# mLSTM values on one core: fp32 products of weights and values replaced by pairs of split fp32r products

## The chip, the core and the metric

The kernel runs on one core of one Trainium2 chip. The metric is the device time of one execution in microseconds. A run here is a timed execution; a profile is one execution taken by the hardware profiler. The engines are TensorE (PE, with its weight loads as PEld), VectorE (DVE), ScalarE (ACT), GpSimd (POOL) and SyncE (SP, which issues the DMAs). They run their own instruction streams in order and wait for each other on semaphores.

## The reference, cut to what matters

The reference is one layer of a hybrid encoder: 512 tokens, 1024 channels, three branches (stick-breaking attention, mLSTM, attention into a memory), gates, an output projection and a layer of 16384 small experts. Only the mLSTM branch bears on the change. It is written chunk by chunk; over the whole sequence it amounts to this, for each of 4 heads of width 128:

```python
dmat = where(causal, bcum[..., :, None] - bcum[..., None, :] + ig[..., None, :], -inf)
w    = einsum('bhtd,bhsd->bhts', q, k) * exp(dmat - m_t[..., None])
num  = einsum('bhts,bhse->bhte', w, v)
den  = sum(w, axis=-1)
h    = num / maximum(abs(den), exp(-m_t))[..., None]
```

The change is in the product of the weighted scores `w` with the values `v`. A column of ones beside the values gives `den` from the same product.

## The kernel before

**Layout.** 512 tokens are 4 tiles of 128 partitions. The projections of the normed input come as items: an item is 16 products of 128 x 512 whose weights (1024 columns) were split into a high part by ACT (`high_w`, L1337) and a low part by POOL (`low_ws`, L491; some by DVE), both fp32r. fp32r is the form that TensorE takes as one product per instruction; a plain fp32 matmul is carried out as two. `SPREAD` and `KEEP` are scale factors that make the high part lose its low bits when it is written as fp32r, so that the low part is the exact rest.

**Stages.** The transposes and most projections end near 166 us. Then come four pairs of attention heads (`for p in range(PAIRS)`, 166 to 255 us), between whose steps PE runs gate items 4 to 16; then mLSTM (255 to 284 us); then the memory attention, the branch projections, and from about 330 us to the end the experts.

**mLSTM.** PE does, for heads (0, 1) and then (2, 3): `ml_scores` of both heads (L991, fp32r, 16 products for each head pair of narrowing width), `gate_item(17)` or `gate_item(19)`, `ml_values` of both heads (L1002), and a further gate item, 18 or 20. The scores stay in PSUM as the causal part only: 1280 columns for each head. Ahead of the values DVE makes the exponents (`decay`, L1900), ACT their exponential (L1470), POOL masks the diagonal blocks (`keep_causal`, L480), and DVE multiplies by the scores (`weigh`, L1951) and signals `w_ready`. `ml_values(h)` waits for `w_ready` and forms 10 products of 128 x 129 for each head: weights `ew[h]`, moving operand `ml_v4`, both plain fp32. `divide(h)` (L1961 to L1966) reads the result, and `num_out` lets PE write the next scores into the same banks.

**What sets the order.** Each engine's stream is written out by hand. The order around the change: on DVE `take_gate` (L1834) copies a gate item out of PSUM, and PE waits for it before the gate item after next; `split_low` (L1908, L1911) makes the low parts of the mLSTM queries and keys, without which `ml_scores` can't run. On ACT `split_high(p)` stands at the end of attention pair p, `high_ws` makes the high part of the next item's weights. On POOL `low_ws` follows the items in order. Lines L1877 to L1960 of the DVE stream hold the attention pairs' loop and the decays.

## Time and profile before

| | |
|---|---|
| time, median of 3 runs | 1466.06 us (1465.7 to 1466.77) |
| the profiled execution's own time | 1466.18 us |
| its span, first to last instruction | 1464.5 us |
| PE busy | 1455.2 us, 99% of the span |
| DVE, ACT, POOL busy | 76%, 51%, 29% |
| mean granted TensorE clock | 0.999 of full speed |

The time is the span and 1.7 us around it. "Busy" of PE is from a product's start to the end of its last result, so that neighbours overlap: the distance from one product's start to the next, not the length of one, tells what a product costs. The rows of a timeline merge neighbours of one line: start, time from the first start to the last end, and how many.

### The profile page before, as it was taken

To read this page: it belongs to the slowest core of one execution; us is meant where nothing else is said; L and a number is where in the kernel's file an instruction comes from. 1 tells how busy PE (TensorE), PEld (TensorE's weight loads), DVE (VectorE), ACT (ScalarE), POOL (GpSimd) and SP (SyncE) were. 2 spreads that over 40 slices of the span, in tenths; PEclk is the share of its full clock that TensorE was granted. 3 is DMA by queue.
4 is the path that set the end of the run, shared out by engine and by line. 5 is a ranking of instruction groups with operands and counts; after the bars stand their busy time and mean duration, and the time that the engine had idled before them with its cause. 6 is when DMAs were issued, how large, how long until landed. Compare 5 with 4: busy or idle time off the path is not lost.

```text
span 1464.5 us, 22288 instructions
## 1 busy us (share of the span) xinstructions
PE 1455.2 (99%) x7466; PEld 1208.1 (82%) x7466; DVE 1107.4 (76%) x1903; ACT 747.2 (51%) x955; POOL 424.6 (29%) x200
## 2 busy tenths in 40 slices
PE   9999999999999999999999999999999999999999
PEld 8888777878788888888888888888888888888887
DVE  5977688867589999996999997346666666666665
ACT  6444677477645454554556555454444444444442
POOL 5866435436546687884000000000000000000000
PEclk9999999999999999999999999999999999999999
DMA  7544533538433666666888888988888888888883
GB/s 239 172 144 144 202 123 108 174 121 300 152 116 115 219 219 208 215 209 206 299 304 303 310 297 305 321 285 287 297 297 281 296 283 296 284 293 286 292 286 139
DMA packets 166705, 345.16 MB, mean 236 GB/s; under 512 B 13420, under 2 KB 78956, under 8 KB 164336
## 3 DMA queue, kind: packets, MB, share of 16 engines
q1 hardware_dynamic: 166640, 344.32, 69.2%
q8 instruction: 37, 0.61, 0.2%
q14 instruction: 28, 0.23, 0.0%
HBM read 268.76 MB, written 75.51 MB: 235 GB/s over the span
## 4 chain that ended last, share of the span: by engine, by line
PE 86%; DVE 10%; ACT 2%; POOL 1%; issue 0%; DMA 0%; SPq 0%; ACTq 0%; POOLq 0%
PE ps L1229 32%; PE ps L1220 25%; PE ps L747 9%; PE ps L770 6%; PE ps L1258 4%; PE ps L1089 3%; DVE top_lists L2156 1%; DVE top_lists L2149 1%; POOL u_r L538 1%; PE ps L954 1%; PE ps L735 1%; DVE top_in L2150 1%; DVE top_lists L2153 1%; DVE top_lists L2146 1%; PE ps L938 1%; PE ps L964 1%
## 5 line engine op out<-in xcount | busy, mean ns | idle before, releaser
L1220 PE MATMUL ps<-hT_r,u_r 128*128 128x512 f32 x2048 | 470.6, 391 | 0.1
L1229 PE MATMUL ps<-v_r,w_pairs 128*128 128x512 f32 x2036 | 461.7, 389 | 0.0
L1220 PEld LDWEIGHTS ps<-hT_r,u_r 128*128 128x128 f32 x2048 | 382.8, 188 | 79.7 <-POOL u_r L538 0.5
L1229 PEld LDWEIGHTS ps<-v_r,w_pairs 128*128 128x128 f32 x2036 | 382.3, 188 | 79.2
L491 POOL TENSOR_TENSOR w_r<-w_raw,w_r 128x1024 fp32r<-128x1024 f32 x85 | 217.0, 2558 | 182.5 <-ACT w_r L1337 105.0
L2295 DVE TENSOR_TENSOR v_r<-vraw,v_r 128x1024 fp32r<-128x1024 f32 x128 | 156.9, 1226 | 148.7 <-ACT v_r L1675 148.7
L1675 ACT ACTIVATE v_r<-vraw 128x1024 fp32r<-128x1024 f32 x128 | 135.7, 1061 | 253.6 <-PE ps L1229 249.0
L1622 ACT ACTIVATE act_stage<-ps 128x512 f32<-128x512 f32 x128 | 76.6, 598 | 226.5 <-PE ps L1220 226.4
L538 POOL TENSOR_TENSOR u_r<-uraw,u_r 128x1024 fp32r<-128x1024 f32 x60 | 172.9, 2892 | 46.6 <-ACT u_r L1603 46.4
L1337 ACT ACTIVATE w_r<-w_raw 128x1024 fp32r<-128x1024 f32 x95 | 100.0, 1059 | 112.2 <-PE ps L747 44.9
L1603 ACT ACTIVATE u_r<-uraw 128x1024 fp32r<-128x1024 f32 x128 | 134.9, 1054 | 15.8 <-DMA uraw<-in_u 12.9
L747 PE MATMUL ps<-xT_r,w_r 128*128 128x512 f32 x592 | 141.2, 393 | 0.0
L747 PEld LDWEIGHTS ps<-xT_r,w_r 128*128 128x128 f32 x592 | 109.8, 188 | 23.3 <-issue 0.7
L2257 DVE TENSOR_TENSOR u_r<-uraw,u_r 128x1024 fp32r<-128x1024 f32 x68 | 82.6, 1223 | 56.1 <-ACT u_r L1603 55.7
L2291 DVE TENSOR_TENSOR w_f<-act_in,g_in 128x512 f32<-128x512 f32 x128 | 87.6, 685 | 6.1 <-issue 6.1
L2298 DVE SCALAR_TENSOR_TENSOR w_pairs<-w_pairs,w_f 128x512 fp32r<-128x512 f32 x128 | 87.5, 684 | 0.0
L1677 ACT ACTIVATE w_pairs<-w_f 128x512 fp32r<-128x512 f32 x128 | 78.6, 614 | 3.8 <-DVE w_f L2291 3.8
L1645 ACT ACTIVATE stage<-ps 128x1024 f32<-128x1024 f32 x64 | 61.8, 1019 | 5.0 <-PE ps L1258 5.0
L1258 PEld LDWEIGHTS ps<-onehots 128*128 128x128 bf16 x1024 | 58.8, 97 | 4.2 <-issue 4.2
L1258 PE MATMUL ps<-onehots 128*128 128x128 bf16 x1024 | 61.6, 219 | 0.0
L770 PE MATMUL ps<-w_r,xT_r 128*128 128x512 f32 x256 | 58.2, 389 | 0.0
L770 PEld LDWEIGHTS ps<-w_r,xT_r 128*128 128x128 f32 x256 | 48.1, 188 | 10.0
(272 smaller groups left out, 1538.6 us busy)
## 6 DMA issues: line engine op xcount, KB each, us to landing
uraw<-in_u SPq DMA_DIRECT2D x128, 512.0 KB, 4.8
vraw<-in_v SPq DMA_DIRECT2D x128, 512.0 KB, 5.2
w_raw<-in_w SPq DMA_DIRECT2D x100, 512.0 KB, 3.5
acts_out<-act_stage SPq DMA_DIRECT2D x128, 256.0 KB, 2.3
gates<-stage SPq DMA_DIRECT2D x16, 2048.0 KB, 7.4
g_in<-gates SPq DMA_DIRECT2D x64, 512.0 KB, 6.4
act_in<-acts_out SPq DMA_DIRECT2D x128, 256.0 KB, 5.2
gates_pre<-pre_stage SPq DMA_DIRECT2D x24, 256.0 KB, 2.4
```

What stands on the lines that cost most here:

```text
L491: pool.tensor_tensor(wr4[:, n % 2, 1, :], raw3[:, n % 4, :], wr4[:, n % 2, 0, :].bitcast(F32), ALU.subtract).then_inc(w_lo_ready, 1)
L538: pool.tensor_tensor(u2[n % 4][:, 1, :], u_raw[n % 4], u2[n % 4][:, 0, :].bitcast(F32), ALU.subtract).then_inc(u_lo, 1)
L747: ins = pe.matmul(bank(b), slot_of(s)[:, w, k * P:(k + 1) * P], act[:, w, k, :], start=k + w == 0, stop=k == KD - 1 and w == 1)
L770: ins = pe.matmul(bank(b0 + t), act[:, w, 2 * j + k, t * P:(t + 1) * P], wr4[:, s, w, k * BANK:(k + 1) * BANK], start=j + k + w == 0, stop ...
L1220: ins = pe.matmul(bank(s % 2), u2[s][:, w, k * P:(k + 1) * P], hr4[:, w, k, :], start=i == 0, stop=i == 15, skip_group_check=True)
L1229: ins = pe.matmul(bank(2 * q + h), w2[:, s, w, q * P:(q + 1) * P], v2[s][:, w, h * BANK:(h + 1) * BANK], start=start and w == 0, stop=stop ...
L1258: ins = pe.matmul(ps[:, at:at + P], oh_tiles[3 * s][:, q // PAIR, :, q % PAIR], oh_tiles[3 * s + 1 + w][:, q // PAIR, :, q % PAIR], start= ...
L1337: act.activation(slot_of(n)[:, 0, :], raw3[:, q, :], ACT.Copy, scale=KEEP).then_inc(w_hi_ready, 1)
L1603: act.activation(u2[s][:, 0, :], u_raw[s], ACT.Copy, scale=KEEP).then_inc(u_hi, 1)
L1675: act.activation(v2[s][:, 0, :], vr[:, s, :], ACT.Copy, scale=KEEP).then_inc(v_hi, 1)
L2291: dve.tensor_tensor(wf[:, s % 2, :].rearrange("p (b t) -> p b t", t=BLK), ai3[:, s, :].rearrange("p (b t) -> p b t", t=BLK), g4[:, par, :, ...
L2295: dve.tensor_tensor(v2[s][:, 1, :], vr[:, s, :], v2[s][:, 0, :].bitcast(F32), ALU.subtract).then_inc(v_lo, 1)
```

## The change

The values' products become fp32r. Weights are split as `ew_hi`, `ew_lo`; values as `ml_v_high`, `ml_v_low`. For each of the 40 blocks there are two products that add up in PSUM: high weights by high values and low weights by low values; the scale of the weights' high part carries the cross terms. The width goes from 129 to 130 columns (two columns of ones). The values are split on ACT and POOL in three runs of 3, 7 and 6 head tiles behind attention pairs 0, 1 and 2. The weights of a head are split once they are made: ACT writes the high part (`high_e`), DVE the low part in place (`low_e`), and `w_ready` is now signalled by `low_e`. On ACT, `high_e(0)` and `high_e(1)` stand ahead of the weights of items 18 and 19, `high_e(2)` and `high_e(3)` between those of items 20 and 21. On DVE `decay(3)` and `take_gate(16)` change places. Some semaphores are merged, a few tiles move by 16 or 288 columns, and two rows change places in memory, so that a split run of values can lie where they were.

```diff
+V_RUNS = (3, 7, 6)
 ...
+            def low_v(i):
+                pool.wait_ge(v_split_hi, i + 1)
+                pool.tensor_tensor(v_run(ml_v_low, i), v_run(ml_v, i), ml_v_high[i].bitcast(F32),
+                                   ALU.subtract).then_inc(v_split_lo, 1)
+
-            low_ws(I_G + GATES_IN_KV, 14)
+            low_ws(I_G + GATES_IN_KV, 5)
+            for p in range(PAIRS - 1):
+                low_v(p)
+                low_ws(I_G + GATES_IN_KV + 5 + 3 * p, 3)
 ...
             def ml_values(h):
+                pe.wait_ge(v_split_lo, len(V_RUNS))
                 pe.wait_ge(w_ready, h + 1)
                 for t in range(TT):
-                    at = (h % 2 * 3 + t // 2) * BANK + (t % 2) * (HD + 1)
+                    at = (h % 2 * 3 + t // 2) * BANK + (t % 2) * (HD + 2)
                     for kt in range(t + 1):
-                        ins = pe.matmul(ps[:, at:at + HD + 1], part(ew[h], kt, t, t + 1), ml_v4[:, kt, h, :],
-                                        start=kt == 0, stop=kt == t)
+                        for w, weights in enumerate((ew_hi[h], ew_lo[h])):
+                            ins = pe.matmul(ps[:, at:at + HD + 2], part(weights, kt, t, t + 1), (v_high, v_low)[w](kt, h),
+                                            start=kt + w == 0, stop=kt == t and w == 1)
 ...
+            def high_v(i):
+                act.activation(ml_v_high[i], v_run(ml_v, i), ACT.Copy, scale=KEEP).then_inc(v_split_hi, 1)
+
+            def high_e(h):
+                act.wait_ge(weighed, h + 1)
+                at_least(act, num_done, h - 1)
+                act.activation(ew_hi[h], ew[h], ACT.Copy, scale=1.0 / SPREAD).then_inc(weighed_hi, 1)
 ...
                 if p < PAIRS - 1:
                     split_high(p)
+                    if p == 0:
+                        act.wait_ge(n_out, 2 * TT)
+                        act.wait_ge(row_in, 32)
+                    high_v(p)
 ...
+            for h in range(2):
+                high_e(h)
             high_ws(I_G + 18, I_G + 19)
             act.activation(ml_o, ml_o, ACT.Sigmoid).then_inc(ml_factors, 1)
-            high_ws(I_G + 20, I_G + 21, I_G + 22)
+            high_ws(I_G + 20)
+            for h in range(2, MLH):
+                high_e(h)
+            high_ws(I_G + 21, I_G + 22)
 ...
             decay(2)
+            decay(3)
             take_gate(16)
-            decay(3)
 ...
-                dve.scalar_tensor_tensor(out=ew[h], in0=region(h % 2), scalar=HD_SCALE * SPREAD, in1=ew[h],
-                                         op0=ALU.mult, op1=ALU.mult).then_inc(w_ready, 1)
+                dve.scalar_tensor_tensor(out=ew[h], in0=region(h % 2), scalar=HD_SCALE * SPREAD * SPREAD, in1=ew[h],
+                                         op0=ALU.mult, op1=ALU.mult).then_inc(weighed, 1)
+
+            def low_e(h):
+                dve.wait_ge(weighed_hi, h + 1)
+                dve.scalar_tensor_tensor(out=ew_lo[h], in0=ew_hi[h].bitcast(F32), scalar=1.0 - SPREAD, in1=ew[h],
+                                         op0=ALU.mult, op1=ALU.add).then_inc(w_ready, 1)
 ...
             for h in (0, 2):
                 weigh(h)
                 weigh(h + 1)
+                low_e(h)
+                low_e(h + 1)
                 take_gate(17 + h)
```

On PE, from the last products of the scores of heads 0 and 1 to the gate item behind their values, before (`L1002` is `ml_values`):

```order
L991 MATMUL ps<-projT_r 128x512
L991 MATMUL ps<-projT_r 128x384
L991 MATMUL ps<-projT_r 128x256
L991 MATMUL ps<-projT_r 128x128
L747 MATMUL ps<-xT_r,w_r 128x512 x16
L1002 MATMUL ps<-ml_v,work 128x129 x20
L747 MATMUL ps<-xT_r,w_r 128x512 x16
```

The same place after the change (`L1029` is `ml_values`; the pair of rows repeats 20 times):

```order
L1016 MATMUL ps<-projT_r 128x128
L772 MATMUL ps<-xT_r,w_r 128x512 x16
L1029 MATMUL ps<-ml_v_high,lk_hi 128x130
L1029 MATMUL ps<-ml_v_low,lk_lo 128x130
L1029 MATMUL ps<-ml_v_high,lk_hi 128x130
L1029 MATMUL ps<-ml_v_low,lk_lo 128x130
```

20 fp32 instructions, which the trace shows as 40 products, became 40 fp32r instructions; what stands around them is the same.

On DVE, from `decay(2)` through the weighing of heads 0 and 1 to `split_low(2)`, before (`L1900` is `decay`, `L1834` `take_gate`, `L1951` `weigh`, `L1908` and `L1911` `split_low`):

```order
L1900 TENSOR_SCALAR work<-r_all,key_cols 128x128
L1834 TENSOR_TENSOR pre_stage<-ps,rstd_b 128x512
L1900 TENSOR_SCALAR work<-r_all,key_cols 128x512
L1900 TENSOR_SCALAR work<-r_all,key_cols 128x384
L1900 TENSOR_SCALAR work<-r_all,key_cols 128x256
L1900 TENSOR_SCALAR work<-r_all,key_cols 128x128
L1951 SCALAR_TENSOR_TENSOR work<-ps,work 128x1280 x2
L1834 TENSOR_TENSOR pre_stage<-ps,rstd_b 128x512
L1908 SCALAR_TENSOR_TENSOR projT_r<-projT_r,projT 128x512
```

And after (`L1946` is `decay`, `L1880` `take_gate`, `L1997` `weigh`, `L2002` `low_e`, `L1954` `split_low`):

```order
L1946 TENSOR_SCALAR work<-r_all,key_cols 128x512
L1946 TENSOR_SCALAR work<-r_all,key_cols 128x384
L1946 TENSOR_SCALAR work<-r_all,key_cols 128x256
L1946 TENSOR_SCALAR work<-r_all,key_cols 128x128
L1880 TENSOR_TENSOR pre_stage<-ps,rstd_b 128x512
L1997 SCALAR_TENSOR_TENSOR work<-ps,work 128x1280 x2
L2002 SCALAR_TENSOR_TENSOR lk_lo<-lk_hi,work 128x1280 x2
L1880 TENSOR_TENSOR pre_stage<-ps,rstd_b 128x512
L1954 SCALAR_TENSOR_TENSOR projT_r<-projT_r,projT 128x512
```

`take_gate(16)` moved behind `decay(3)`, and the two `low_e` stand between `weigh` and `take_gate(17)`.

On ACT, from `split_high(3)` to the copies of the memory attention's queries, after the change (`L1511` is the exponential, `L1486` `high_e`, `L1364` `high_w`, `L1517` the sigmoid):

```order
L1511 ACTIVATE work<-work 128x1280 x3
L1486 ACTIVATE lk_hi<-work 128x1280 x2
L1364 ACTIVATE w_r<-w_raw 128x1024 x2
L1517 ACT_TABLE_LOAD
L1517 ACTIVATE ml_o<-ml_o 128x2048
L1364 ACTIVATE w_r<-w_raw 128x1024
L1486 ACTIVATE lk_hi<-work 128x1280 x2
L1364 ACTIVATE w_r<-w_raw 128x1024 x2
```

Both `L1486` rows are new; the weights of items 18 and 19, and of item 21, now stand behind them.

## Rows read from the trace of the kernel before

**Rows 1.** The page: busy time by engine, and the last chain's shares by engine.

```profile
PE 1455.2 (99%) x7466; PEld 1208.1 (82%) x7466; DVE 1107.4 (76%) x1903; ACT 747.2 (51%) x955; POOL 424.6 (29%) x200
...
PE 86%; DVE 10%; ACT 2%; POOL 1%; issue 0%; DMA 0%; SPq 0%; ACTq 0%; POOLq 0%
```

**Rows 2.** Groups by line and shape, 150 to 330 us: count, busy us, mean ns.

```profile
L1002 PE MATMUL ps<-ml_v,work 128*128 128x129 f32 x80 | 9.3, 275 | 0.0
...
L1002 PEld LDWEIGHTS ps<-ml_v,work 128*128 128x128 f32 x80 | 9.2, 192 | 0.2
```

**Rows 3.** Timeline of PE in mLSTM: start us, length us, line, names, count.

```profile
257.75 3.89 PE L747 MATMUL ps<-xT_r,w_r 128*128 128x512 f32 x16
261.48 4.63 PE L1002 MATMUL ps<-ml_v,work 128*128 128x129 f32 x40
265.86 3.91 PE L747 MATMUL ps<-xT_r,w_r 128*128 128x512 f32 x16
...
275.85 4.63 PE L1002 MATMUL ps<-ml_v,work 128*128 128x129 f32 x40
280.23 3.91 PE L747 MATMUL ps<-xT_r,w_r 128*128 128x512 f32 x16
```

**Rows 4.** Timeline of PE, fp32r products of the last attention head, narrow ones among them.

```profile
244.16 0.22 PE L954 MATMUL ps<-lk_hi,rest_r 128*128 128x128 f32 x1
244.22 0.28 PE L954 MATMUL ps<-lk_hi,tri_r 128*128 128x128 f32 x1
244.33 0.44 PE L954 MATMUL ps<-lk_lo,tri_r 128*128 128x512 f32 x1
244.62 0.34 PE L954 MATMUL ps<-lk_lo,ones_r 128*128 128x384 f32 x1
```

**Rows 5.** Timeline of PE's weight loads in the same stretch.

```profile
244.05 0.19 PEld L954 LDWEIGHTS ps<-lk_hi,rest_r 128*128 128x128 f32 x1
244.16 0.19 PEld L954 LDWEIGHTS ps<-lk_hi,tri_r 128*128 128x128 f32 x1
244.28 0.19 PEld L954 LDWEIGHTS ps<-lk_lo,tri_r 128*128 128x128 f32 x1
244.39 0.19 PEld L954 LDWEIGHTS ps<-lk_lo,ones_r 128*128 128x128 f32 x1
```

**Rows 6.** Timeline of DVE in mLSTM.

```profile
256.05 1.36 DVE L1900 TENSOR_SCALAR work<-r_all,key_cols 128x512 f32<-128x512 f32 x4
257.33 2.88 DVE L1951 SCALAR_TENSOR_TENSOR work<-ps,work 128x1280 f32<-128x1280 f32 x2
...
262.29 2.81 DVE L1908 SCALAR_TENSOR_TENSOR projT_r<-projT_r,projT 128x512 fp32r<-128x512 f32 x1
...
271.10 2.89 DVE L1951 SCALAR_TENSOR_TENSOR work<-ps,work 128x1280 f32<-128x1280 f32 x2 [0.32 <-PE ps L991]
276.05 0.69 DVE L1834 TENSOR_TENSOR pre_stage<-ps,rstd_b 128x512 f32<-128x512 f32 x1 [2.06 <-PE ps L747]
```

**Rows 7.** Timeline of ACT in mLSTM.

```profile
257.45 1.28 ACT L1470 ACTIVATE work<-work 128x1280 f32<-128x1280 f32 x1 [1.38 <-DVE work L1900]
258.63 1.04 ACT L1337 ACTIVATE w_r<-w_raw 128x1024 fp32r<-128x1024 f32 x1
...
274.27 1.06 ACT L1337 ACTIVATE w_r<-w_raw 128x1024 fp32r<-128x1024 f32 x1 [5.17 <-PE ps L747]
```

**Rows 8.** Timeline of POOL in mLSTM.

```profile
259.83 4.71 POOL L491 TENSOR_TENSOR w_r<-w_raw,w_r 128x1024 fp32r<-128x1024 f32 x2
```

**Rows 9.** Timelines of ACT and POOL at the end of attention pair 2.

```profile
227.65 0.62 ACT L1449 ACTIVATE projT_r<-projT 128x512 fp32r<-128x512 f32 x1
230.85 1.24 ACT L1426 ACTIVATE work<-ps 128x1280 f32<-128x1280 f32 x1 [2.58 <-PE ps L942]
...
228.05 2.35 POOL L491 TENSOR_TENSOR w_r<-w_raw,w_r 128x1024 fp32r<-128x1024 f32 x1 [0.56 <-PE ps L747]
```

**Rows 10.** Instructions on the tile r_all: its DMA's issue, us.

```profile
L592 SPq DMA_DIRECT2D r_all<-acts_out x1: 432/432/432, 151.8 to 151.8; - x1
```

More of the change, by code:

```diff
@@ L276, in build, with v_high, v_low, v_run @@
         sb_v3 = sb_v.rearrange("p (t c) -> p t c", c=512)
-        ml_v4 = ml_v.rearrange("p (t h c) -> p t h c", t=TT, c=HD + 1)
+        ml_v4 = ml_v.rearrange("p (t h c) -> p t h c", t=TT, c=HD + 2)
+        def v_high(t, h):
+            n = t * MLH + h
+            i = 0 if n < V_RUNS[0] else 1 if n < V_RUNS[0] + V_RUNS[1] else 2
+            at = (n - sum(V_RUNS[:i])) * (HD + 2)
+            return ml_v_high[i][:, at:at + HD + 2]
+        def v_low(t, h):
+            return ml_v_low[:, (t * MLH + h) * (HD + 2):(t * MLH + h + 1) * (HD + 2)]
+        def v_run(whole, i):
+            return whole[:, sum(V_RUNS[:i]) * (HD + 2):sum(V_RUNS[:i + 1]) * (HD + 2)]
         ml_o3 = ml_o.rearrange("p (t c) -> p t c", c=512)
@@ L294, in build @@
         ew = lk + aw
+        ew_hi = [lkr[0][h % 2] for h in range(MLH)]
+        ew_lo = [lkr[1][0], lkr[1][1], aw_r[:, 0:CAUSAL], aw_r[:, CAUSAL:2 * CAUSAL]]
         probs = [work[:, 0:1024], work[:, 1024:2048]]
@@ L300, in row @@
             return rows[0:4, n * T:(n + 1) * T]
-        r_abs, r_f, r_lf, r_b, r_a, r_max, r_m, r_zero = (row(n) for n in range(8))
+        r_abs, r_f, r_lf, r_b, r_a, r_m, r_max, r_zero = (row(n) for n in range(8))
         r_all3 = r_all.rearrange("p (h t) -> p h t", t=T)
@@ L1403, in _ @@
             high_w(I_N + 2, (I_N + 2) % 4)
-            act.activation(r_abs, r_abs, ACT.Ln, bias=1.0).then_inc(if_ln, 1)
+            act.activation(r_abs, r_abs, ACT.Ln, bias=1.0).then_inc(if_made, 1)
             for b in range(4):
```

81 lines of the change are left out of this document (42 added, 39 removed).

## The prediction, as it was made before the changed kernel ran

> **What bounds the kernel now.** I read the page first [rows 1]: PE is busy 99% of the span and holds 86% of the chain that ended last. So time is won only if PE's own stream gets shorter, and lost only if PE is made to wait. The groups by line and shape come next [rows 2]: the products to be replaced are 80 records of 128 x 129 in fp32, two for each of the 40 instructions, each with a weight load of its own. The timeline of PE [rows 3] gives their real price. The values of heads 0 and 1 start at 261.48 and the gate item behind them at 265.86: 4.38 us for 40 products, 0.110 us each; heads 2 and 3 take the same 4.38 us. Together 8.76 us, and no stage of the change touches PE elsewhere. Even if these products cost nothing, the kernel would win 0.6%; a measurement of this kernel can tell about 0.2%, or 2.9 us, from no change.
>
> **What the new products cost.** The program order shows 80 fp32r instructions of 128 x 130. An fp32r instruction is one record in the trace (a gate item has 16 instructions and 16 records [rows 3]), so 80 records replace 80 records. The only saving can come from the rate: fp32r streams its columns faster than fp32. But each product needs its own 128 x 128 weights, and these are again fp32r. What does a narrow fp32r product cost when its neighbour is narrow too? The trace of before has no long run of them, but it has pairs, at the end of each attention head's suffix sums. There the second narrow product starts 0.06 us after the first (244.16, 244.22), and the next one 0.11 us after that (244.33) [rows 4]. The weight loads of the same stretch start at 244.05, 244.16, 244.28 and 244.39 [rows 5]: 0.34 us for three, 0.113 each. The last of them could have begun at 244.33, when the product before it did, and began 0.06 us later: the load ahead of it was not done. And the 512-wide product at 244.33 takes 0.29 us to its successor at 244.62, where 512-wide ones in a gate item are (261.48 - 257.75) / 16 = 0.233 apart [rows 3]. So it, too, waited some 0.06 us for its weights. I read from this that an fp32r weight load occupies the load path for 0.11 us, whatever the product beside it, and that a run of products narrower than that (0.06 us) goes at the pace of its loads. The fp32 products of before stream for about as long as a load takes, which is why their loads are 0.11 us apart as well [rows 2, 3].
>
> The bounds for one product are then 0.107 (a little under the mean load distance) and 0.113 us. For 80 products: 8.56 to 9.04 us against 8.76, that is -0.2 to +0.3 us. I take 0.112, since three loads in a row measured it: 80 x 0.112 = 8.96, **+0.2 us**. [...]
>
> The Trainium skill has two rules here that disagree. Its page "TensorE: Matmul & The Clock Gate", section "LDWEIGHTS (loading the stationary operand)", gives a load's time as its column count over 1.2 GHz, 107 ns for 128 columns; the loads in rows 5 agree within 6 ns. The section "Back-to-back issue gap" of the same page gives 81 ns for a sustained 128-wide product with its load; the rows speak against it for fp32r, but no run of them is long, so it is a rival below.
>
> **The splits of the values.** ACT gets three copies of 390, 910 and 780 columns, POOL three subtractions of the same size. By the ACT copy of 1024 columns at 1.04 us [rows 7] the largest costs 0.9 us. They stand behind `split_high` of pairs 0 to 2, where ACT idles: in pair 2 it is free from 228.27 to 230.85, 2.58 us [rows 9], and 0.8 us are put there; pairs 0 and 1 end with the same steps and about as much room. Were this cover gone, ACT's start on the next pair would slip by up to that 0.9 us. The first copy waits for the broadcast of `r_all`, whose DMA was issued at 151.8 [rows 10], 35 us ahead of pair 0's end: nothing. On POOL a subtraction of 1024 columns takes 2.35 us [rows 9], so 0.9, 2.1 and 1.8 us, behind the low part of items 8, 11 and 14; after item 14's, at 230.40, POOL has nothing to do until ACT has made the next pair's high weights, ten us later. Queued behind `low_v` are the low weights of the next items, which have not got their high parts by then. PE's wait for `v_split_lo` is over some 29 us before it is asked. **Zero.**
>
> **The split of the weights.** This is the part on the path: `w_ready` used to follow `weigh`, and now follows `weigh`, `high_e` and `low_e`. Heads 0 and 1, walked through with durations of before: `decay(3)` (1.36 us) no longer stands between `take_gate(16)` and `weigh(0)`; it fits ahead, where DVE waited for gate item 16 to end at 255.3. `take_gate(16)`, a copy of 0.69 us, then ends near 256.8, and `weigh(0)`, which started at 257.33, can follow it [rows 6]. Two `weigh` take 2.88 us, 1.44 apart: to 258.2 and 259.7. `high_e` is an ACT pass over 1280 columns, 1.28 us [rows 7]: 258.3 to 259.6 and 259.8 to 261.0; ACT is free for it, since the exponential of head 3, which ran at 257.45, comes a good microsecond earlier with the swap. `low_e(0)` follows at 259.7 and takes as long as `weigh`, to 261.2; `low_e(1)` to 262.6. PE asks for head 0 at 261.48 and for head 1 2.2 us later at 263.7 [rows 3]. **Slack 0.3 us and 1.1 us.** Heads 2 and 3: `weigh` at 271.10 to 273.99, `high_e` to 274.0 and 275.4, `low_e` to 275.6 and 277.0; PE asks at 275.85 and 278.0: slack 0.2 and 1.0 us.
>
> **What is queued behind them.** On ACT the high weights of item 18 move from 258.63 [rows 7] to about 261.0, those of 19 to 262.0; POOL's low parts, which ran from 259.83 to 264.54 [rows 8], follow at about 262.1 to 264.5 and 266.9. Gate item 18 begins at 265.86 and needs its low part 1.9 us later; item 19 comes 6 us after it. Item 21's high part slips from 274.27 to 275.4, its gate item comes after 286. On DVE `take_gate(17)` slips by about 1 us and `split_low(2)` with it. That one is the place where two engines collide: before, the first half of `split_low(2)`, 512 columns, took 2.81 us where a copy of 512 columns takes 0.69 [rows 6], since it stood still until POOL's subtraction ended at 264.54 [rows 8]. Now item 18's subtraction ends at about the same time, so `split_low(2)` ends near 266, as before, and `divide(0)` and `divide(1)` are done near 267.7 and 269.3; PE asks for the first at 269.6 with `ml_scores(2)`, for the second and for `split_low(3)` at 270.9. `low_e` reads two tiles of SBUF and could be held up by POOL in the same way, but in both places POOL has nothing to run: item 18's subtraction needs ACT's copy, which stands behind `high_e(1)`, and item 21's that behind `high_e(3)`. **Zero, with 0.3 us to spare at the tightest.**
>
> **The sum.** 1466.18 + 0.2 = 1466.4 for an execution like the profiled one. That one was 0.1 above the median of the runs before (1466.06), so **1466.3 us** as a median: no change.
>
> **Rivals.**
> - *The products stream at their own rate.* If loads were hidden, a product would cost 0.06 us, as the second narrow one does [rows 4]: 80 x (0.110 - 0.058) = 4.2 us, 1461.9. For it: the 0.06 itself, and fp32r is what all of the big stages use. Against it: each 0.06 is followed by a 0.11 and a stretched product. Chance 0.07.
> - *A product in between*, with a load that is partly hidden: halfway, 0.085, gives 80 x 0.025 = 2.0 us, 1464.1; no row shows such a distance. The skill's 81 ns, a figure of the section named above, would make it 2.3 us, 1463.8. Chance 0.04; within 0.2% either way.
> - *Slower: load and product in turn.* If in a long run of narrow products a load could not start until the product before it has left the array, each costs a load and a product, 0.11 + 0.055 = 0.165 us: 80 x 0.055 = +4.4 us, 1470.6. It decides from 0.146 us for a product. The rows speak against it: the load at 244.16 starts with the product before it, not after [rows 4, 5]. The skill says on the page named above, Part 3, "The mechanism", that a load overlaps running products only when its row group differs; rows 4 and 5 show loads of full height that do overlap. Chance 0.03.
> - *Slower: the weights come late.* If POOL is in the way of a `low_e` for one of its subtractions (2.35 us) less the slack, PE stands for 2.0 us: 1468.2, still no change by the measure; if in both places, 1470.2. Chances 0.03 and 0.01.
> - *The change is not what it says:* the compiler carries out each fp32r product as two. Then 160 products: +9 us, 1475. The gate items speak against it. Chance 0.01.
>
> **How the numbers follow.** The forecast has 0.81. The time is its time, 1466.3. Its own spread is the -0.2 to +0.3 of the products, up to 0.5 us where a slack of 0.2 or 0.3 is used up, and the 1.1 us between the runs shown. The range reaches from 1464.5, below which stand only the hidden and the half-hidden loads (0.11), to 1468.5, above which stand loads in turn, two late weights and split products (0.05). Faster by over 0.2%: 0.07. Slower by over 0.2%: 0.03 + 0.01 + 0.01 = 0.05. Within: 0.88.
>
> **What would show it right or wrong.** In the timeline of PE after, the values should take 4.4 to 4.5 us for each head pair, with product starts and load starts both 0.11 us apart; a distance of 0.06 means the first rival, 0.165 the third. The lengths of the products should be near 275 ns although they stream half as long, because each waits for its weights. DVE's `low_e` should end 0.2 to 0.3 us before PE starts the values, and no idle row of PE should name it. `split_low(2)` should end near 266. What would make the prediction wrong: that a long run of narrow loads behaves unlike the three that I could see, or that the chain from `weigh` to `low_e` is longer than the sum of its parts by more than its slack, since PE would then stand at both places and nothing later gives it back.

## The result, and the profile after

The changed kernel takes 1468.73 us (median of 14 runs, 1466.84 to 1470.17), the kernel before, on the same chip, 1465.46 us (14 runs, 1463.45 to 1466.79). The ratio is 1.0025, with a 95% interval of 1.0018 to 1.0033: slower by a quarter of a per cent; the medians are 3.3 us apart. (The ratios in this text are those on record. They are not quotients of the medians beside them and can differ from these by some 0.05%.) The forecast was 1466.3, no change, with a range up to 1468.5. The profiled execution took 1469.57 us and has a span of 1467.8 us, 3.3 us more than before.

The page of the changed kernel, busy time by engine and the shares of the chain that ended last, against [rows 1]:

```profile
PE 1455.5 (99%) x7466; PEld 1208.2 (82%) x7466; DVE 1115.5 (76%) x1907; ACT 754.5 (51%) x962; POOL 433.6 (30%) x203
...
PE 84%; DVE 11%; ACT 2%; POOL 1%; issue 1%; DMA 0%; SPq 0%; ACTq 0%; POOLq 0%; DVEq 0%
```

PE's busy time has grown by 0.3 us only, while the span grew by 3.3: by this row 3.0 us are time in which PE stood. 2.33 of them are the wait that is shown below; 0.7 lie in the first 20 us, where PE is busy 16.30 us and was 17.01, far from the change. The chain agrees: two points went from PE to DVE and to issue. DVE is busy 8.1 us longer, ACT 7.3, POOL 9.0: the splits, and on DVE and POOL also time in which an instruction counts as busy while it is held up.

Where PE stood is seen in its timeline (start us, length us, line, names, count; in brackets the idle time ahead and what ended it). `L772` is a gate item, `L1016` `ml_scores`, `L1029` `ml_values`:

```profile
265.34 3.85 PE L772 MATMUL ps<-xT_r,w_r 128*128 128x512 f32 x16
269.18 1.49 PE L1016 MATMUL ps<-projT_r 128*128 128x512 f32 x8
273.01 1.50 PE L1016 MATMUL ps<-projT_r 128*128 128x512 f32 x8 [2.33 <-DVE projT_r L1957]
274.31 5.45 PE L772 MATMUL ps<-xT_r,w_r 128*128 128x512 f32 x16
...
284.01 3.86 PE L772 MATMUL ps<-xT_r,w_r 128*128 128x512 f32 x16
```

The same timeline, the first and last products of the values:

```profile
260.93 0.22 PE L1029 MATMUL ps<-ml_v_high,lk_hi 128*128 128x130 f32 x1
260.99 0.28 PE L1029 MATMUL ps<-ml_v_low,lk_lo 128*128 128x130 f32 x1
261.10 0.28 PE L1029 MATMUL ps<-ml_v_high,lk_hi 128*128 128x130 f32 x1
...
279.60 0.22 PE L1029 MATMUL ps<-ml_v_high,lk_hi 128*128 128x130 f32 x1
```

I compare one stretch throughout, called the stage below: from the first product of the values of heads 0 and 1 to the start of gate item 20, behind the values of heads 2 and 3. Before it is 280.23 - 261.48 = 18.75 us [rows 3], after it is 284.01 - 260.93 = 23.08: 4.33 us more. By pieces, from start to start:

| piece of the stage | before | after | difference |
|---|---|---|---|
| values of heads 0, 1 | 4.38 | 4.41 | +0.03 |
| gate item 18 | 3.75 | 3.84 | +0.09 |
| scores of heads 2, 3 | 2.51 | 5.13 | **+2.62** |
| gate item 19 | 3.73 | 5.28 | **+1.55** |
| values of heads 2, 3 | 4.38 | 4.41 | +0.03 |

So the new products cost what the old ones did. Two other things happened. Between `ml_scores(2)` and `ml_scores(3)` PE stood for 2.33 us by its timeline, waiting for `split_low(3)` on DVE (`L1957`). Then gate item 19, whose products didn't change, took 1.55 us longer. The windows of the gate item's line give the reason (stretch, its length, PE and PEld busy with counts, granted clock, DMA share, GB/s):

```profile
274.31:277.73 3.42, 3.42 (x8) 2.74 (x9) 0.50 0.73 230
277.73:279.60 1.87, 1.87 (x9) 1.31 (x7) 1.00 0.00 0
```

For the first 3.42 us, 8 products, the granted clock was 0.50, which is 1.2 GHz; after that it was back at 1.00, 2.4 GHz. 8 products in 3.42 us are 0.427 each, where products at full clock are 0.233 apart: 8 x 0.194 = 1.55 us. Before the clock fell PE had stood still for 2.33 us and then formed the eight products of `ml_scores(3)`, from 273.01 to 274.31, still at the full clock.

Why was `split_low(3)` late? DVE's timeline from `low_e` on (`L2002`; `L1880` is `take_gate`, `L1954` and `L1957` the two halves of `split_low`, `L2017` the last step of a `divide`), against [rows 6]:

```profile
259.01 2.90 DVE L2002 SCALAR_TENSOR_TENSOR lk_lo<-lk_hi,work 128x1280 fp32r<-128x1280 f32 x2
261.82 0.68 DVE L1880 TENSOR_TENSOR pre_stage<-ps,rstd_b 128x512 f32<-128x512 f32 x1
262.42 2.27 DVE L1954 SCALAR_TENSOR_TENSOR projT_r<-projT_r,projT 128x512 fp32r<-128x512 f32 x1
264.62 2.87 DVE L1957 TENSOR_TENSOR projT_r<-projT,projT_r 128x512 fp32r<-128x512 f32 x1
...
269.63 1.13 DVE L2017 TENSOR_SCALAR y_ml<-ps,den 128x128 f32<-128x128 f32 x4
270.68 1.58 DVE L1954 SCALAR_TENSOR_TENSOR projT_r<-projT_r,projT 128x512 fp32r<-128x512 f32 x1
272.18 0.68 DVE L1957 TENSOR_TENSOR projT_r<-projT,projT_r 128x512 fp32r<-128x512 f32 x1
```

And POOL's, the low weights of items 18 and 19 and then of item 20, against [rows 8]:

```profile
261.49 5.45 POOL L508 TENSOR_TENSOR w_r<-w_raw,w_r 128x1024 fp32r<-128x1024 f32 x2 [3.58 <-ACT w_r L1364]
269.34 2.37 POOL L508 TENSOR_TENSOR w_r<-w_raw,w_r 128x1024 fp32r<-128x1024 f32 x1 [2.40 <-PE ps L772]
```

Half of a `split_low` takes 0.68 us when nothing is in its way. In the stage there are four halves, and three are stretched: 2.27, 2.87 and 1.58 us. Each of their ends can be set against the end of a subtraction. Taken singly, the two that POOL's row merges last 2.65 us from 261.49 and 2.83 from 264.11. The first half ends at 264.69, 0.55 us behind the end of the first subtraction (264.14); the second at 267.49, 0.55 behind the second (266.94); and 272.26 is 0.55 behind the end of item 20's (271.71). So such a half stands until the subtraction is over and then does its own work. Before, one half was stretched, to 2.81 us, again 0.56 beyond the end of POOL's work at 264.54, and the other came behind it and took its 0.68. From its first start to its last end `split_low(2)` takes 5.1 us, before 3.4; `split_low(3)` loses 0.9 us, before nothing. That POOL is busy here is ACT's doing:

```profile
257.70 2.68 ACT L1486 ACTIVATE lk_hi<-work 128x1280 fp32r<-128x1280 f32 x2 [0.90 <-DVE work L1997]
260.29 1.99 ACT L1364 ACTIVATE w_r<-w_raw 128x1024 fp32r<-128x1024 f32 x2
```

`high_e(0)` and `high_e(1)` now stand ahead of the high weights of items 18 and 19, so that these are made from 260.29 instead of 258.63, back to back, and POOL's two subtractions start at 261.49 instead of 259.83. In this profile everything here runs 0.55 us ahead of the profile of before (the values start at 260.93, before at 261.48). Counted from the values' start, the high weights and the subtractions come 2.2 us later than before, and `split_low(2)` (262.42, before 262.29) 0.7 us later. Before, the second subtraction had begun when the first half came, and nothing stood behind it; now the first half meets the first subtraction, and the second half the second.

From the values' start to the end of `split_low(3)` it is 11.9 us, before 8.7: 3.2 more. 2.2 of them are the second half of `split_low(2)`, 0.9 are `split_low(3)`'s own wait for item 20's subtraction. Before, 0.7 us of this were slack (`split_low(3)` ended at 270.18, half of the scores was through near 270.87); the other 2.5 make up nearly all of the 2.62 us lost in the scores.

The Trainium skill has this collision on its page "SBUF — State Buffer", section "Who interferes with whom": a DVE instruction with two SBUF inputs and a GpSimd instruction that reads SBUF exclude each other, and the later one waits for the whole of the earlier. The rows above agree: both halves of `split_low` read two tiles of SBUF and are stretched, while `take_gate` and `divide`, which read PSUM, ran at their usual 0.68 and 1.13 us. It holds the other way round too: `low_e(1)` ran until 261.91, so that the first subtraction stood behind it from 261.49, and the second behind the first half: 2.65 and 2.83 us, where one alone takes 2.35 [rows 9].

### The profile page after: what moved, and what is told of

It reads as the page before. It is cut to its first block, busy times and chain, and to the rows that moved or that the text cites. A ratio compares the mean times of both kernels' runs of the same rounds, so it can differ in the third digit from the quotient of the medians.

```text
span 1467.8 us, 22293 instructions
## 1 busy us (share of the span) xinstructions
PE 1455.5 (99%) x7466; PEld 1208.2 (82%) x7466; DVE 1115.5 (76%) x1907; ACT 754.5 (51%) x962; POOL 433.6 (30%) x203
## 4 chain that ended last, share of the span: by engine, by line
PE 84%; DVE 11%; ACT 2%; POOL 1%; issue 1%; DMA 0%; SPq 0%; ACTq 0%; POOLq 0%; DVEq 0%
PE ps L1256 31%; PE ps L1247 25%; PE ps L772 9%; PE ps L795 6%; PE ps L1285 4%; PE ps L1116 3%; DVE top_lists L2209 1%; DVE top_lists L2202 1%; POOL u_r L563 1%; PE ps L979 1%; PE ps L760 1%; DVE top_in L2203 1%; DVE top_lists L2206 1%; DVE top_lists L2199 1%; PE ps L963 1%
## 5 line engine op out<-in xcount | busy, mean ns | idle before, releaser
L1364 ACT ACTIVATE w_r<-w_raw 128x1024 fp32r<-128x1024 f32 x95 | 99.8, 1058 | 105.5 <-PE ps L772 41.3
L772 PE MATMUL ps<-xT_r,w_r 128*128 128x512 f32 x592 | 142.7, 396 | 0.0
L772 PEld LDWEIGHTS ps<-xT_r,w_r 128*128 128x128 f32 x592 | 111.0, 190 | 23.6 <-issue 0.7
```

Source lines behind the costliest of these rows:

```text
L772: ins = pe.matmul(bank(b), slot_of(s)[:, w, k * P:(k + 1) * P], act[:, w, k, :], start=k + w == 0, stop=k == KD - 1 and w == 1)
L1364: act.activation(slot_of(n)[:, 0, :], raw3[:, q, :], ACT.Copy, scale=KEEP).then_inc(w_hi_ready, 1)
```

## The experiments

**Theory.** ACT's new passes shift POOL's subtractions onto `split_low(2)`; each half waits for one of them; `divide(0)`, `divide(1)` and `split_low(3)` follow late; PE stands; the clock falls. **Rivals.** (a) DVE simply has too much work in this stretch, 2.9 us of `low_e` for each pair, and the collision adds nothing; (b) the new products themselves, or the splits of the values, cost the time; (c) the slow gate item has a cause of its own, unrelated to PE's standing still.

### `split_low(2)` moved ahead

Both halves of `split_low(2)` are taken out of the stretch and put behind `minus_abs(3)`, where its inputs have long been ready. Nothing else is changed, so DVE has the same work in all.

```diff
                 minus_abs(p)
+                if p == PAIRS - 1:
+                    split_low(2)
                 take_gate(m)
 ...
-                if h == 0:
-                    split_low(2)
                 divide(h)
```

> The changed kernel with split_low(2) moved into attention pair 3, behind minus_abs(3), where DVE idled 2.2 us in the profile of before. If the loss is PE's stall ahead of ml_scores(3) and the clock that falls behind it, both go: no wait of PE for split_low, granted clock 1.00 through mLSTM, the values of heads 2 and 3 start 4.3 us earlier relative to those of heads 0 and 1 (14.4 us apart instead of 18.7), and the time is 4.3 us under the changed kernel's, about 1464.5, equal to before within 0.1%. If the loss is spread over the kernel (tiles at other places, a later start), the time stays near 1468.7.

Measured: 1464.20 us (11 runs), kernel before 1465.23 (33 runs), ratio 0.9994 (0.9985 to 1.0003). PE's timeline has the scores in one piece and the gate item at its usual length, and the granted clock over 255 to 285 us is 1.00:

```profile
268.05 2.67 PE L1016 MATMUL ps<-projT_r 128*128 128x512 f32 x16
270.56 3.89 PE L772 MATMUL ps<-xT_r,w_r 128*128 128x512 f32 x16
```

DVE's and POOL's timelines:

```profile
266.20 0.68 DVE L1954 SCALAR_TENSOR_TENSOR projT_r<-projT_r,projT 128x512 fp32r<-128x512 f32 x1
```

```profile
260.51 5.00 POOL L508 TENSOR_TENSOR w_r<-w_raw,w_r 128x1024 fp32r<-128x1024 f32 x2 [3.58 <-ACT w_r L1364]
```

The half seen here is the first of `split_low(3)`, now unhindered: POOL is done at 265.5. The stage takes 18.76 us. The whole loss is gone, 4.3 of 4.3 us in the stage. This doesn't yet separate the theory from rival (a), since the move takes at least 1.4 us of DVE work out of the stretch as well.

### The same move in the kernel before

> Control: the kernel before with the same move of split_low(2). PE waits for nothing there before, so by the theory nothing is won: time within 0.1% of before, and the move in e1 wins only because it undoes the stall. If the move is worth something by itself (over 0.15%), e1's gain can't all be put down to the stall.

Measured: 1464.55 us (11 runs) against 1465.23, ratio 0.9998 (0.9988 to 1.0007); the stage takes 18.75 us. The move by itself wins nothing. What it took away in the changed kernel was the stall, not something that was there before.

### POOL waits for `split_low(2)`

The DVE stream is the changed kernel's, word for word. Only POOL's second subtraction waits until both halves of `split_low(2)` are through.

```diff
-            low_ws(I_G + 18, I_PQ - 1 - I_G - 18)
+            low_ws(I_G + 18, 1)
+            pool.wait_ge(ml_split_lo, 6)
+            low_ws(I_G + 19, I_PQ - 1 - I_G - 19)
```

> The changed kernel with POOL waiting for split_low(2) to be done before the low part of item 19. DVE has the same work in the same order. Port theory (each half of split_low(2) stands still behind one of POOL's two subtractions in a row): the second half now takes 0.7 us instead of 2.87, divide(0) starts 2.1 us earlier, PE's stall shrinks from 2.5 us to under 0.6, the clock doesn't fall, time 3.5 to 4.3 us under the changed kernel. Queue theory (DVE simply has 2.9 us more to do ahead of split_low(2)): the stall stays over 1.5 us and the time within 1 us of the changed kernel's.

Measured: 1464.68 us (10 runs), ratio 1.0001 (0.9992 to 1.0011); stage 18.76 us. DVE's and POOL's timelines:

```profile
261.56 2.27 DVE L1956 SCALAR_TENSOR_TENSOR projT_r<-projT_r,projT 128x512 fp32r<-128x512 f32 x1
263.75 0.68 DVE L1959 TENSOR_TENSOR projT_r<-projT,projT_r 128x512 fp32r<-128x512 f32 x1
```

```profile
260.55 2.73 POOL L508 TENSOR_TENSOR w_r<-w_raw,w_r 128x1024 fp32r<-128x1024 f32 x1 [3.50 <-ACT w_r L1366]
264.74 2.40 POOL L508 TENSOR_TENSOR w_r<-w_raw,w_r 128x1024 fp32r<-128x1024 f32 x1 [1.46 <-DVE projT_r L1959]
```

This is the run that decides. DVE has the same instructions in the same order, the first half is stretched just as in the changed kernel, and only the second, 2.87 us, is back at 0.68. With these 2.2 us the 0.9 us of `split_low(3)` have gone as well (both halves take 0.68), and with them the stall. Rival (a) is out. The first half again ends 0.55 us behind its subtraction (263.83 and 263.28).

### PE kept at work while it waits

Ahead of `ml_scores(3)` PE forms ten fp32 products of constants into a free bank. They change no result.

```diff
                 at_least(pe, num_out, h - 1)
+                if h == 3:
+                    pe.wait_ge(y_out, PAIRS)
+                    for i in range(10):
+                        pe.matmul(bank(6)[:, 0:P], neg_ones[:, :], neg_ones[:, :], start=True, stop=True)
                 pe.wait_ge(ml_split_lo, 2 * h + 2)
```

> The changed kernel with 10 fp32 products of 128 x 128 of constants into a free bank, ahead of PE's wait for split_low(3): 2.2 us of work in the stall, nothing else changed. If the fall of the clock to half is caused by the stall, the clock stays at 1.00 from 273 to 279 us, gate item 19 takes 3.7 us instead of 5.3, ml_scores(3) starts where it did (within 0.1 us), and the time is 1.5 us under the changed kernel's. If the clock falls for another reason (the fp32r products at half load ahead of it), it falls again and nothing is won.

Measured: 1467.25 us (10 runs), ratio 1.0016 (1.0007 to 1.0025). PE's timeline, and the windows row of 255 to 285 us (busy time with counts of PE, PEld, DVE, ACT, POOL, granted clock, DMA share, GB/s; `L1020` is `ml_scores` here and `L1016` the filler):

```profile
270.07 1.49 PE L1020 MATMUL ps<-projT_r 128*128 128x512 f32 x8
271.71 2.50 PE L1016 MATMUL ps<-neg_ones 128*128 128x128 f32 x20
273.96 1.46 PE L1020 MATMUL ps<-projT_r 128*128 128x512 f32 x8
275.26 3.89 PE L772 MATMUL ps<-xT_r,w_r 128*128 128x512 f32 x16
```

```profile
255.00:285.00 30.00, 29.85 (x191) 26.68 (x190) 28.22 (x49) 14.76 (x12) 13.66 (x16) 1.00 0.36 114
```

`ml_scores(3)` starts no earlier than in the changed kernel, 3.89 us behind `ml_scores(2)` where it was 3.83, so the wait is all there. But the clock stays at 1.00 and gate item 19 takes 3.73 us (start to start) instead of 5.28. The stage is 21.58 us: 1.5 of the 4.3 us are won by useless work. That speaks against rival (c), but it is one profile, and the fall doesn't happen in each run of the changed kernel either (see below). The timed runs point the same way without deciding: their ratio's interval, 1.0007 to 1.0025, overlaps the changed kernel's, 1.0018 to 1.0033.

### The values' product without the split of the weights

`high_e` and `low_e` are gone; `weigh` writes fp32r directly and both products of a block use it. The split of the weights is left out, so the result has lower precision; the products and the splits of the values stay.

```diff
-            for h in range(2):
-                high_e(h)
             high_ws(I_G + 18, I_G + 19)
 ...
-                low_e(h)
-                low_e(h + 1)
 ...
-                        for w, weights in enumerate((ew_hi[h], ew_lo[h])):
+                        for w, weights in enumerate((ew_lo[h], ew_lo[h])):
```

> The changed kernel without the split of the weights: no high_e on ACT, no low_e on DVE, both products of a block take the weights as weigh writes them, in fp32r (so the split's arithmetic is left out). PE's products, the values' splits and the swap of decay(3) stay. If the products cost what fp32's did and the splits of the values are hidden, and the loss comes from the weights' split alone, the time is that of before within 0.1%, with no stall of PE. If the fp32r products or the values' splits cost something of their own, the time stays over before by that.

Measured: 1464.84 us (10 runs) against 1464.48 (15 runs), ratio 1.0004 (0.9994 to 1.0013). The values take 4.42 us per pair, PE does not wait, the stage is 18.80 us. With the change's 80 products and all of its work on the values, the time is that of before within the measurement. Rival (b) is out.

### Only ACT's passes, in the kernel before

The opposite direction: two copies of 1280 columns are put on ACT ahead of the high weights of item 18, with DVE's order of `decay(3)` and `take_gate(16)` as in the change. DVE gets no `low_e`, PE keeps its fp32 products.

```diff
             decay(2)
+            decay(3)
             take_gate(16)
-            decay(3)
 ...
+            for h in range(2):
+                act.wait_ge(w_ready, h + 1)
+                act.activation(lkr[0][h % 2], ew[h], ACT.Copy, scale=1.0 / SPREAD)
             high_ws(I_G + 18, I_G + 19)
```

> The kernel before with the swap of decay(3) and take_gate(16) and with two passes of 1280 columns on ACT at the place of high_e(0) and high_e(1), their results unused. DVE gets no work. ACT's weights of items 18 and 19 come 2.5 us later and so do POOL's two subtractions. Port theory: both halves of split_low(2) stand behind a subtraction, its second half ends near 267, divide(0), divide(1) and split_low(3) slip by 1.5 to 2.2 us, PE stalls 1 to 2.5 us ahead of ml_scores(3); time 1 to 4 us over before. Queue theory (DVE's added passes are the cause): no stall, time as before.

Measured: 1468.77 us (6 runs) against 1464.48, ratio 1.0030 (1.0017 to 1.0043); the stage takes 23.09 us, the changed kernel's 23.08. Timelines of DVE, POOL and PE (`L1911`, `L1914` are `split_low`, `L991` `ml_scores`):

```profile
260.87 2.66 DVE L1911 SCALAR_TENSOR_TENSOR projT_r<-projT_r,projT 128x512 fp32r<-128x512 f32 x1
263.46 2.87 DVE L1914 TENSOR_TENSOR projT_r<-projT,projT_r 128x512 fp32r<-128x512 f32 x1
```

```profile
260.62 5.16 POOL L491 TENSOR_TENSOR w_r<-w_raw,w_r 128x1024 fp32r<-128x1024 f32 x2 [3.58 <-ACT w_r L1337]
```

```profile
272.16 2.11 PE L991 MATMUL ps<-projT_r 128*128 128x512 f32 x8 [2.55 <-DVE projT_r L1914]
```

Both halves are stretched, PE waits 2.55 us for the same instruction, and the clock falls again (0.94 over 255 to 285 us). So 2.7 us of work on an engine that is half idle makes the whole loss, with no new work on DVE or PE.

### Half the width

The values' products form 66 of the 130 columns; the rest of the result is left out. If they ran at the rate of their columns they would take half as long.

```diff
-                            ins = pe.matmul(ps[:, at:at + HD + 2], part(weights, kt, t, t + 1), (v_high, v_low)[w](kt, h),
+                            ins = pe.matmul(ps[:, at:at + 66], part(weights, kt, t, t + 1), (v_high, v_low)[w](kt, h)[:, 64:130],
```

> The changed kernel with the values' products cut from 130 to 66 moving columns (half of the values' columns are left out), weights and order as they are. Load theory: product starts stay 0.112 us apart, 4.4 to 4.5 us for a head pair. Streaming theory: 0.03 to 0.06 us less each, 2 us or more less for a head pair.

Measured in one run: 1471.69 us. The first 40 products take 4.38 us, as with 130 columns (4.41), so it is the weight loads that they wait for. The time is worse, though, than the changed kernel's. The stall is there as before (2.35 us), and the clock falls twice; windows of four stretches:

```profile
270.00:273.00 3.00, 0.95 (x3) 0.89 (x4) 3.00 (x4) 0.00 (x0) 0.76 (x1) 0.86 0.00 0
273.00:276.00 3.00, 3.00 (x12) 2.62 (x11) 2.25 (x2) 1.27 (x1) 0.00 (x0) 0.57 0.54 186
...
279.00:283.00 4.00, 4.00 (x35) 4.00 (x35) 2.20 (x8) 0.00 (x0) 2.32 (x1) 0.92 0.65 193
283.00:287.00 4.00, 4.00 (x12) 3.32 (x13) 2.98 (x8) 0.00 (x0) 0.00 (x0) 0.50 1.01 400
```

The second fall, near 282.4 us, comes in the middle of the values of heads 2 and 3 with no wait ahead of it: from there their products are 0.21 us apart instead of 0.11. That I had not expected, and the next run asks for it.

### Half the width, without the stall

> Part of the work is left out: the values' products form 66 of 130 columns, as in the run of half the width, but split_low(2) stands behind minus_abs(3), so PE does not stall. Theory (the clock falls because PE stood still): values 4.38 to 4.42 us for each pair, product starts 0.11 apart, no wait, clock 1.00 from 255 to 330, time near 1464.5. Rival (narrow products by themselves leave TensorE so little active that the clock falls): clock under 1.00 behind the first or the second values although no stall stands there, time 1467 or more.

Measured in one run: 1467.51 us. No row of PE names a wait in the stage, and yet the clock falls in the middle of the first values (windows, then PE's timeline):

```profile
262.00:265.00 3.00, 3.00 (x21) 3.00 (x20) 1.63 (x7) 2.44 (x2) 3.00 (x2) 0.67 0.54 168
265.00:268.00 3.00, 3.00 (x9) 2.52 (x10) 2.28 (x9) 0.00 (x0) 0.41 (x1) 0.50 0.23 94
```

```profile
262.92 0.31 PE L1029 MATMUL ps<-ml_v_high,lk_hi 128*128 128x66 f32 x1
263.04 0.40 PE L1029 MATMUL ps<-ml_v_low,lk_lo 128*128 128x66 f32 x1
263.26 0.40 PE L1029 MATMUL ps<-ml_v_high,lk_hi 128*128 128x66 f32 x1
```

My theory, that the clock falls only where PE stands, has fallen. The distance of the products goes from 0.11 to 0.21 us, the stage takes 21.97 us with nothing to wait for. A run of products of 66 columns, each waiting for its weights, was enough. In this execution it happened at the first values and not at the second; in the run before at the second and not at the first. So whether it happens varies, and I can't say from two executions how often. With 130 columns, no profile without a stall (`split_low(2)` moved, POOL waiting, no split of the weights) shows a fall there.

### Wide products: values as weights

The roles are exchanged: a block of values is loaded as weights and the split weights move through in one go, 512, 384, 256 and 128 columns wide. 8 loads for a head instead of 20. The result comes out transposed and the columns of ones, which give the denominators, are left out, so what DVE divides and stores is not the mLSTM's.

```diff
-                for t in range(TT):
-                    at = (h % 2 * 3 + t // 2) * BANK + (t % 2) * (HD + 2)
-                    for kt in range(t + 1):
-                        for w, weights in enumerate((ew_hi[h], ew_lo[h])):
-                            ins = pe.matmul(ps[:, at:at + HD + 2], part(weights, kt, t, t + 1), (v_high, v_low)[w](kt, h),
-                                            start=kt + w == 0, stop=kt == t and w == 1)
+                for w, weights in enumerate((ew_hi[h], ew_lo[h])):
+                    for kt in range(TT):
+                        ins = pe.matmul(causal(h % 2, kt), (v_high, v_low)[w](kt, h)[:, 0:P], part(weights, kt),
+                                        start=w == 0 and kt != 3, stop=w == 1, skip_group_check=True)
```

> The changed kernel with the operands of the values' products swapped: values as weights, the split weights as moving operand of 512, 384, 256 and 128 columns, 8 products for a head instead of 20 (the output is the transpose, which the rest of the kernel does not expect; the divisions run on it as they are). The columns streamed are the same 1280 a head and part. If narrow products were bound by their weight loads, a head pair takes 2.5 us, as the scores' 16 products of the same widths do, instead of 4.5, and its second head's product starts are 0.17 to 0.23 us apart for the wide ones. If it was the streaming that bound them, it stays at 4.4 to 4.5 us.

Measured in one run: 1466.44 us. The values take 2.50 us per pair instead of 4.41. But PE comes 1.9 us earlier to work that isn't ready:

```profile
262.63 3.88 PE L772 MATMUL ps<-xT_r,w_r 128*128 128x512 f32 x16
268.42 2.06 PE L1016 MATMUL ps<-projT_r 128*128 128x512 f32 x8 [1.90 <-DVE y_ml L2015]
271.34 2.58 PE L1016 MATMUL ps<-projT_r 128*128 128x512 f32 x8 [0.86 <-DVE projT_r L1955]
273.72 4.92 PE L772 MATMUL ps<-xT_r,w_r 128*128 128x512 f32 x16
```

It waits 1.90 us for `divide(0)` and 0.86 for `split_low(3)`, and the clock falls (0.89 over 255 to 285 us). It falls between the two: it was 1.00 until 269.0, and then (PE and PEld busy with counts, DVE, ACT, POOL, clock, DMA share, GB/s):

```profile
269.00:270.40 1.40, 1.40 (x7) 1.20 (x5) 1.40 (x5) 0.00 (x0) 0.01 (x1) 0.53 0.00 0
```

So the wait of 1.90 us was enough, with products at full clock for 0.6 us behind it. The stage takes 20.84 us, 2.24 less than the changed kernel's and still 2.09 more than before.

### Wide products, without the stall

The same with `split_low(2)` moved ahead as in the first experiment.

> Part of the work is changed: the values' product is formed transposed, with the values as weights and the split weights as the moving operand (32 wide products for each head pair instead of 80 loads of 128x128 blocks), so the divided output is not the mLSTM's; and split_low(2) stands behind minus_abs(3), as in the run that took the stall away. Theory (the stall behind POOL is what stops any gain in the values from arriving): values 2.50 us for each head pair instead of 4.41, scores 2.51 with no wait, gate item 19 3.73, clock 1.00, so 2 x 1.9 = 3.8 us under before, ratio 0.997. Rival A (the gain is hidden anyway, the next wait ends as late): PE stands ahead of ml_scores(2) for divide(0) or divide(1), and the ratio stays within 0.999 to 1.000. Rival B (PE leans on DVE's weigh and low_e once its own stream is shorter): the second values start 14.3 us or more behind the first, ratio about 0.9985.

Measured: 1461.48 us (9 runs) against 1464.47 (12 runs), ratio 0.9974 (0.9964 to 0.9984). The stage takes 14.96 us, 3.79 less than before; the expectation was 3.8 (its count of the products is wrong: they are 16 for each head pair, 32 in all). Neither rival came true: PE's timeline has no wait, and the second values start 12.47 us behind the first. The granted clock is 1.00. The medians differ by 3.0 us only; I can't say where the other 0.8 went.

```profile
265.79 2.67 PE L1016 MATMUL ps<-projT_r 128*128 128x512 f32 x16
268.30 3.89 PE L772 MATMUL ps<-xT_r,w_r 128*128 128x512 f32 x16
```

So there is time to win in this place, but only in a form with few loads, and only once POOL and DVE no longer collide. Is it fp32r's or only the fewer loads'? The wide form with plain fp32 products was not run. The trace of before has wide fp32 products elsewhere, in the memory attention (PE's timeline; the row behind it starts at 302.04):

```profile
300.32 1.88 PE L1066 MATMUL ps<-work,mem_v 128*128 128x512 f32 x4
```

These are 0.43 us apart, fp32r ones of the same width 0.233 [rows 3]. By that, my estimate for 2 x 2 x 1280 columns of a head pair in fp32 is 4.3 us, as much as the 4.38 of before: the wide form would win nothing without fp32r. A kernel that uses it needs the denominators and the normalisation behind it in the transposed layout; that was not built.

## Why the prediction was wrong

The stages of eight profiles side by side (us from the first values to gate item 20):

| kernel | stage | scores of heads 2, 3 | gate item 19 |
|---|---|---|---|
| before | 18.75 | 2.51 | 3.73 |
| changed | 23.08 | 5.13 | 5.28 |
| changed, `split_low(2)` moved | 18.76 | 2.51 | 3.73 |
| changed, POOL waits | 18.76 | 2.51 | 3.73 |
| changed, PE kept at work | 21.58 | 5.19 with the filler | 3.73 |
| changed, no split of the weights | 18.80 | 2.51 | 3.74 |
| before, with ACT's two passes | 23.09 | 5.87 | 4.70 |
| changed, wide products, `split_low(2)` moved | 14.96 | 2.51 | 3.73 |

**What the new products cost: right.** 0.112 us for each was forecast, +0.2 us in all. It was 2 x 4.41 = 8.82 us for 80, 0.110 each, +0.06. The starts are 0.11 apart, the lengths 0.28, and only the first pair has the 0.06 that three loads of the last attention head had shown [rows 4]. Half the width in the same time shows that it is the loads.

**The splits of the values: right.** Without the split of the weights, and with these splits, the ratio is 1.0004 (0.9994 to 1.0013).

**The split of the weights: right for PE.** `low_e` for heads 0 and 1 ran from 259.01 to 261.91. The two together take 2.90, so the first was done near 260.5, and PE started its head at 260.93: a slack of 0.4 to 0.5 us where 0.3 was forecast. No row of PE names `low_e`. The sentence that POOL has nothing to run beside a `low_e` was wrong, by the prediction's own times as well (`low_e(1)` until 262.6, the subtraction from 262.1). It cost nothing here because POOL came second and was the one to wait.

**What is queued behind them: wrong, and this is the step that failed.** The times of POOL's subtractions were forecast well: 262.1 to 266.9, measured 261.49 to 266.94, which is 262.0 to 267.5 when counted from the same start of the values as before; each measured time of this paragraph is 0.55 us later by that count. The sentence that fell is that `split_low(2)` "ends near 266, as before". I had one half of it wait for item 18's subtraction and let the other pass, as in the trace of before. But there the other half passed because POOL had run out of work at 264.54. Now item 19's subtraction stood ready, and the second half waited for that one too: it ended at 267.49. From there the slip passes down DVE's queue undiminished. `divide(1)` was forecast to end at 269.3 and ended at 270.8, 1.5 us late like `split_low(2)`, 2.0 by the common start. `split_low(3)`, due near 270.5 by the same reckoning (two halves of 0.6 behind `divide(1)`), then met item 20's subtraction and ended at 272.86. PE had `ml_scores(2)` behind it at 270.67, and "0.3 us to spare" became a wait of 2.33 us. The numbers for this stood in the prediction, in the same paragraph: the two subtractions follow each other without a gap until 266.9. What I didn't do was to ask the same question of the second half.

**The clock: not in the prediction at all.** Every price of a wait in it is the wait's own length. Here 2.33 us of standing still were followed by 8 products at 1.2 GHz, 1.55 us more. In the timed runs the two parts can be told apart roughly. A fall like the profile's, 3.42 us at half, would by itself bring the mean clock of a run down to 0.9988, printed as 0.999. In 3 of the 14 runs the mean was 1.000, so in these the clock didn't fall, or for under 1.5 us; they took 1466.84 to 1467.53 us, 1.2 to 1.9 us under the median (the clock in the first 20 us, see the last section, has a share in that). Six runs of the kernel with the filler have a mean of 1.000 too, and took about the same, 1466.55 to 1467.52.

**The sum.** 2.62 + 1.55 + 0.15 for the rest is the stage's 4.33 us. The medians differ by 3.3 only. Part of this is that the fall doesn't happen in each run (not in 3 of the 14, as above); in the profiled execution the stage also began 0.55 us earlier than before.

**The rivals.** (Their times start partly from 1466.1 and partly from 1466.2, which changes no chance.) The right mechanism was among them and on the wrong instruction: "if POOL is in the way of a `low_e`" had the right engine, the right price (2.0 us, against 2.2 lost on DVE) and the right sign, at chances of 0.03 and 0.01. Its price, 1468.2, would have been near the result of 1468.73, but partly by luck: the wait alone, without the clock, is seen in the three runs near 1467.1. The upper end of the range, 1468.5, was passed by 0.2 us, and for that the clock was missing as well.

## What to carry to other kernels

When a step is moved, ask of every instruction in the affected queues, one by one, which transfer or which instruction of a neighbour it will now meet; an engine that worked twice in a row without a gap can hold up two instructions of its neighbour in a row. Price a wait of TensorE of some 2 us with what the clock may take behind it: in this kernel that was 1.55 us behind 2.33. And before narrow products are made cheaper by their rate, look at the distance of their weight loads: here 80 loads cost the same in fp32 and fp32r, and exchanging the operands so that there were 32 loads gave 3.8 us in the stage.

## What the runs showed of the hardware that I had not expected

- A DVE operation with two tiles of SBUF as input, started beside a POOL subtraction, ended 0.55 us behind it: 2.27, 2.87 and 1.58 us instead of 0.68. The next one waited for the next subtraction, although both stood in one queue. POOL pays too when it comes second: its two subtractions took 4.71 us where none of DVE's came between [rows 8], 5.16 with a half of `split_low` between them (before, with ACT's two passes), 5.00 behind the end of a `low_e` (`split_low(2)` moved), and 5.45 with both.
- In four kernels the granted clock fell behind a wait. It went to 0.50 behind one of 2.33 us and 1.3 us of products, and came back after 3.42 us of wide products. It fell as well behind waits of 2.35 and 2.55 us, and behind one of 1.90 us. In 3 of the changed kernel's 14 timed runs it did not fall as in the profile.
- It fell without any wait, in a run of products of 66 columns whose loads were 0.11 us apart. At 130 columns no profile shows that without a wait. What decides between them the runs leave open.
- In some executions the clock is lower in the first 20 us: in 5 of the 12 profiles (before, before with the move, changed, filler, no split of the weights). In the seven others the values start 0.8 to 2.3 us earlier. In the profile of the changed kernel these are the windows

```profile
0.00:10.00 10.00, 6.75 (x36) 6.52 (x37) 2.92 (x8) 3.71 (x10) 2.50 (x15) 0.90 0.72 257
10.00:20.00 10.00, 9.55 (x70) 8.77 (x68) 9.66 (x18) 8.86 (x20) 7.70 (x16) 0.93 1.01 374
```

  and with `split_low(2)` moved both are at 1.00. That is why single executions are compared by their stage and kernels by their medians.
